# The last block of a hybrid decoder step: who weights, roots and scales the final rows

## The reference, cut to what matters

```python
def rmsnorm(x, g):
    return (_rms_f32(x) * g.astype(jnp.float32)).astype(x.dtype)   # x * rsqrt(mean(x*x) + EPS) * g

y = h + moe(hn, w_router, b_router, w_gate_up, b_gate_up, w_down, b_down)
y_prompt, y_sample = rmsnorm(y_prompt, g_final), rmsnorm(y_sample, g_final)
```

## Time and profile before

| | us |
|---|---|
| median of three runs | 1386.02 |
| the profiled execution, its own time | 1385.96 |
| its span, first to last instruction | 1384.1 |
| PE busy | 1352.9 (98%) |
| DVE busy | 1209.8 (87%) |
| ACT busy | 1091.7 (79%) |
| POOL busy | 1010.1 (73%) |

### The profile page before, as it was taken

How to read it: one execution, slowest core, us unless ns; L and a number is a source line. 1 busy time by engine, 2 the same in 40 slices (tenths; PEclk the granted TensorE clock), 3 DMA queues, 4 the chain that set the end, 5 groups by cost and what they waited for, 6 DMA issues and landing times.

```text
span 1384.1 us, 19701 instructions
## 1 busy us (share of the span) xinstructions
PE 1352.9 (98%) x6762; PEld 994.0 (72%) x6762; DVE 1209.8 (87%) x1092; ACT 1091.7 (79%) x1149; POOL 1010.1 (73%) x431
## 2 busy tenths in 40 slices
PE   8999999999999999999999999999999999999995
PEld 5988655667777777777777777777777777777773
DVE  5466556899999999999999999999999999999996
ACT  5354423778888888888888888888888888888885
POOL 2122211266699999899999998999999989999943
PEclk9999999999999999999999999999999999999998
DMA  9522272999999999999999999999999999999984
GB/s 354 189 66 72 88 276 70 367 394 356 372 351 377 378 369 382 372 392 379 377 393 373 378 382 375 379 384 365 389 380 365 381 390 374 382 371 386 375 313 150
DMA packets 51803, 458.99 MB, mean 332 GB/s; under 512 B 11450, under 2 KB 15516, under 8 KB 26122
## 3 DMA queue, kind: packets, MB, share of 16 engines
q1 hardware_dynamic: 40089, 438.33, 80.9%
q0 software_dynamic: 10000, 18.19, 6.0%
q10 hardware_dynamic: 1648, 1.65, 0.4%
HBM read 446.62 MB, written 22.08 MB: 339 GB/s over the span
## 4 chain that ended last, share of the span: by engine, by line
PE 77%; DMA 3%; DVE 1%; issue 1%; POOL 1%; ACT 0%; POOLq 0%; ACTq 0%; DVEq 0%
PE psum L2371 24%; PE psum L2373 24%; PE psum L2372 24%; DMA area<-hn_tbl,idx_i 3%; PE psum L2355 2%; PE psum L2366 2%; POOL small L810 0%; DVE low L1690 0%; PE psum L2342 0%; DVE area L1812 0%; POOL area L695 0%; DVE area L1772 0%; DVE ring L1836 0%; DVE area L1765 0%; POOL out L820 0%
## 5 line engine op out<-in xcount | busy, mean ns | idle before, releaser
L1690 DVE TENSOR_TENSOR low<-raw,high 128x2048 fp32r<-128x2048 f32 x384 | 875.1, 2310 | 35.9 <-ACT high L1098 35.8
L1098 ACT CAST high<-raw 128x2048 fp32r<-128x2048 f32 x384 | 727.8, 1913 | 23.7 <-PE psum L2373 19.2
L2371 PE MATMUL psum<-high,area_r 128*104 128x512 f32 x1536 | 610.4, 397 | 2.5 <-DVE area_r L1754 1.4
L2373 PE MATMUL psum<-low,area_r 128*104 128x512 f32 x1536 | 604.3, 393 | 0.0
L2372 PE MATMUL psum<-high,area_r 128*104 128x512 f32 x1536 | 603.9, 393 | 0.0
L668 POOL PARTITION_BROADCAST brow<-brow x192 | 382.8, 2074 | 41.1 <-DMA brow<-in_biases 40.6
L2373 PEld LDWEIGHTS psum<-low,area_r 128*104 128x104 f32 x1536 | 258.0, 168 | 96.5
L2371 PEld LDWEIGHTS psum<-high,area_r 128*104 128x104 f32 x1536 | 258.0, 168 | 95.0 <-DVE area_r L1754 1.6
L2372 PEld LDWEIGHTS psum<-high,area_r 128*104 128x104 f32 x1536 | 258.3, 168 | 90.7
L737 POOL DMA_INDIRECT area<-hn_tbl,idx_i x32 | 162.9, 5089 | 79.5 <-DVE idx_i L1657 40.8
L665 POOL COPY arrived<-cst 1x1 f32 x60 | 199.5, 3325 | 0.3
(11 more groups left out here) (269 smaller groups left out, 1175.5 us busy)
## 6 DMA issues: line engine op xcount, KB each, us to landing
raw<-in_w_gate_up SPq DMA_DIRECT2D x128, 2048.0 KB, 11.1
raw<-in_w_down SPq DMA_DIRECT2D x64, 2048.0 KB, 11.7
ring<-in_w_in SPq DMA_DIRECT2D x7, 1024.0 KB, 15.3
ring<-in_x_prompt SPq DMA_DIRECT2D x8, 512.0 KB, 9.7
ring<-in_w_out SPq DMA_DIRECT2D x7, 512.0 KB, 4.6
ring<-in_w_mem_kv SPq DMA_DIRECT2D x2, 1024.0 KB, 9.3
ring<-in_mem_kT SPq DMA_DIRECT2D x1, 2048.0 KB, 8.5
ring<-in_cache_mem_v SPq DMA_DIRECT2D x1, 2048.0 KB, 8.2
```

The costliest lines, as they stand in the source:

```text
L1098: nc.scalar.copy(high_w(i), raw_w(t)).then_inc(sem("w_high"), 1)
L1690: v.tensor_tensor(low_w(t), raw_w(t), high_w(i), ALU.subtract).then_inc(sem("w_low"), 1)
L2371: mm(bank, high, wh, start=False, stop=False, skip_group_check=True)
L2373: return mm(bank, high, wl, start=False, stop=stop, skip_group_check=True)
```

## The change

- POOL, between its gather and its roots, multiplies tiles 0 and 1 by `gfin` (128x1024 each); DVE no longer does.
- The five roots are three instructions: tile 2; tiles 3 and 4; tiles 0 and 1. For that `ssf` is set to 1 once, early in the program, so that unused rows of tile 4's column hold a number.
- DVE takes tile 2's mean ahead of `swiglu` of the second half, and scales tile 2 directly behind `swiglu`, ahead of `act_low` and the last `low` part. The means of tiles 0 and 1 stand together in front of the scaling of tiles 3 and 4.
- The last rows: DVE multiplies them by `gfin` into a new buffer `yw` while ACT squares; the scaling by the root is then shared, columns 0 to 511 by DVE, 512 to 1023 by ACT. The scatter waits for both.

```diff
 # ROOTS: first tile, behind the last tile, how many means must be there
+        ROOTS = ((2, 3, 1), (3, 5, 3), (0, 2, 5))
 # SP, store_rows
-                        sp.wait_ge(sem("yf_ready"), NTT * again + j + 1)
+                        sp.wait_ge(sem("yf_ready"), 3 * again + j - 1)
 # POOL, rows_last
-                for s, j in enumerate(ROW_ORDER):
-                    pool.wait_ge(sem("ssf_ready"), NTT * (times - 1) + s + 1)
-                    nc.gpsimd.tensor_tensor(rsf[0:ROWS[j], j:j + 1], ssf[0:ROWS[j], j:j + 1], mh[0:ROWS[j], 0:1],
+                for j in range(2):
+                    pool.wait_ge(sem(f"ld_y{j}"), 16 * times)
+                    nc.gpsimd.tensor_tensor(yg[j], yf[:, j, :], gfin, ALU.mult).then_inc(sem("yg_ready"), 1)
+                for first, last, ready in ROOTS:
+                    pool.wait_ge(sem("ssf_ready"), NTT * (times - 1) + ready)
+                    nc.gpsimd.tensor_tensor(rsf[:, first:last], ssf[:, first:last], mh[:, first:last],
                                             ALU.pow).then_inc(sem("rsf_ready"), 1)
 # ACT, last_squares
+                ac.wait_ge(sem("yw_ready"), 1)
+                ac.wait_ge(sem("rsl_ready"), 1)
+                nc.scalar.activation(yl[0:CAP, 512:1024], yw[0:CAP, 512:1024], ACT.Copy, scale=rsl[0:CAP, 0:1]).then_inc(sem("yl_half"), 1)
 # DVE, last_rows
+                dv.wait_ge(sem("yl_sum"), 2)
+                v.tensor_tensor(yw[0:CAP, :], yl[0:CAP, :], gfin[0:CAP], ALU.mult).then_inc(sem("yw_ready"), 1)
                 dv.wait_ge(sem("ssl_raw"), 2)
 ...
-                v.scalar_tensor_tensor(out=yl[0:CAP, :], in0=yl[0:CAP, :], scalar=rsl[0:CAP, 0:1], in1=gfin[0:CAP],
-                                       op0=ALU.mult, op1=ALU.mult).then_inc(sem("yl_ready"), 1)
+                v.tensor_scalar(yl[0:CAP, 0:512], yw[0:CAP, 0:512], rsl[0:CAP, 0:1], None, ALU.mult).then_inc(sem("yl_ready"), 1)
 # DVE, period, last
+                    if last and i == 6:
+                        row_means(2, 1)
                     if i == 6:
                         swiglu(n, 1)
                     if last and i == 6:
-                        row_means(2, 1)
-                        row_weights(0, 1)
-                        row_weights(1, 1)
+                        row_scale(2, 1)
```

More of the change, by code:

```diff
@@ L271, in build @@
         yl = view(ring, (NTT + 2) * D, [D])
+        yw = view(ring, (NTT + 3) * D, [D])
         yg = (xg[:, 1, :], yrow[:, 1, :])
         ROW_ORDER = (2, 3, 4, 0, 1)
+        ROOTS = ((2, 3, 1), (3, 5, 3), (0, 2, 5))
+        ROOT_OF = {j: i + 1 for i, (first, last, ready) in enumerate(ROOTS) for j in range(first, last)}
         wr = wr_t[:, :].rearrange("p (k e) -> p k e", k=KD)
@@ L819, in last_store @@
                 pool.wait_ge(sem("yl_ready"), 1)
+                pool.wait_ge(sem("yl_half"), 1)
                 nc.gpsimd.indirect_dma_start(y_out[:, :], last_slots, yl[0:CAP, :], None,
@@ L832, in _ @@
                         period(it * UB + (NE + u), u, overflow=True)
+                pool.wait_ge(sem("gathered"), (NE + EXTRA + 2) * 16)
                 rows_last(NE + EXTRA, 2)
@@ L1159, in row_root @@
             def row_root(j, times):
[L1161 to L1162 removed]
+                ac.wait_ge(sem("yg_ready"), 2 * (times - 1) + j + 1)
+                ac.wait_ge(sem("rsf_ready"), len(ROOTS) * (times - 1) + ROOT_OF[j])
                 nc.scalar.activation(yg[j], yg[j], ACT.Copy, scale=rsf[:, j:j + 1]).then_inc(sem("ssf_raw"), 1)
@@ L1539, in _ @@
                 v.tensor_copy(us[:, c, :, 0:2], src)
+            v.memset(ssf, 1.0)
             v.memset(eid_i[:, EXTRA:EXTRA + 1], 0).then_inc(sem("eid_zero"), 1)
@@ L1803, in row_scale @@
                 n = ROWS[j]
-                dv.wait_ge(sem("rsf_ready"), NTT * (times - 1) + ROW_ORDER.index(j) + 1)
+                dv.wait_ge(sem("rsf_ready"), len(ROOTS) * (times - 1) + ROOT_OF[j])
                 v.scalar_tensor_tensor(out=yf[0:n, j, :], in0=yf[0:n, j, :], scalar=rsf[0:n, j:j + 1], in1=gfin[0:n],
                                        op0=ALU.mult, op1=ALU.mult).then_inc(sem("yf_ready"), 1)
[L1808 to L1812, removed]
             def rows_final(times):
-                row_scale(2, times)
                 row_means(0, times)
+                row_means(1, times)
                 row_scale(3, times)
-                row_means(1, times)
                 row_scale(4, times)
@@ L1894, in _ @@
                 row_means(2, 2)
-                row_weights(0, 2)
-                row_weights(1, 2)
+                row_scale(2, 2)
                 row_means(3, 2)
```

## The result

The changed kernel takes 1394.21 us (median of six runs, 1391.85 to 1396.71), the kernel before on the same chip 1385.77 (six runs, 1385.04 to 1387.04). The ratio is 1.0063, 95% interval 1.0053 to 1.0073: slower by 8.4 us. On another chip it gave 1393.52 against 1385.79, ratio 1.0054 (1.0041 to 1.0068). The forecast was 1391.2 in a range of 1386.7 to 1393.0: the direction was right, the size 3 us too small. The profiled execution took 1394.27 us, span 1392.5.

The account below looks back on a forecast made before the run. The scatter's start was taken as the bound, set by the late stores and the last rows behind PE's last matmul. +5.8 (PE) +2.0 (clock) -1.3 (last rows) -1.2 (store path) gave +5.3: 1391.2 us, range 1386.7 to 1393.0.

Parts of the forecast that it names:

- PE restarts later: PE's restart for its last 24 matmuls, behind act_low: 1368.8 instead of 1363.01, +5.8 us.
- clock at half: PE's clock falls during its idle time and stays at half for 3 to 4 us: +2.0 us, lower bound 0.
- last rows: Weighting beside ACT's squares and scaling shared with ACT: 4.1 us instead of 5.4, -1.3 us, bounds 0 and -1.6.
- last rows ready to scatter: Store path before POOL's scatter, late before, now level with the last rows: -1.2 us.
- ahead of the stretch: Time before swiglu's last DVE instruction starts, from where runs are measured to the scatter's start: forecast 0.
- POOL is not free for 8.7 us: POOL stays occupied 8.7 us behind the configuration instruction after the gather; first multiplication at 1362.4.
- The multiplications: POOL's multiplications of tiles 0 and 1: 1.9 us each, 1362.4 to 1366.2; with 2.35 each, +0.9 us.
- first rival: POOL free before 1360.2: PE +3.5, idle 4.3 us, no clock fall; 1387.5 to 1388.6 us; chance 0.18.
- The store path: Stores of tiles 0 to 4 free the scatter at 1379.8 to 1381.0, level with last rows: -1.2 us.
- The memset: Setting ssf early on DVE, some 0.1 us where DVE is not the bound: nothing to +0.2 us.
- The rivals: POOL free before 1360.2: 1387.5 to 1388.6, 0.18; POOL taking DVE's port: 1386.0 to 1387.4, 0.09; root early: 1383.1 to 1383.8, 0.07.

Follow-up runs that it names:

- f1: The kernel before plus a tiny unused POOL multiplication ahead of the gather, so the configuration change stands there: 1385.84 us, ratio 0.9997.
- f2: The changed kernel plus a tiny unused POOL multiplication ahead of the gather, so the configuration change stands there: 1388.85 us, ratio 1.0026.
- g1: The changed kernel plus 27 unused small matmuls on PE ahead of its last 24 matmuls: 1392.23 us, ratio 1.0048.
- g0: The changed kernel run again, unaltered, on g1's chip: 1393.52 us, ratio 1.0054 to the kernel before.
- e2: The changed kernel with POOL taking tile 2's root ahead of its two multiplications: 1390.36 us, ratio 1.0028 to the kernel before.
- e4: The kernel before with only tile 2's scaling moved ahead of act_low: 1387.67 us, ratio 1.0014.
- h2: The changed kernel with its memset of ssf moved behind the routing: 1392.74 us, ratio 1.0047 to the kernel before.
- f3: The changed kernel plus 48 unused small matmuls on PE ahead of its last 24 matmuls: 1393.76 us, ratio 1.0058.
- h1: The kernel before with only the early memset of ssf added: 1385.94 us, ratio 1.0000.
- e1: The changed kernel with tile 2 scaled behind the last low part again: 1390.56 us, ratio 1.0034 to the kernel before.
- e3: The changed kernel with both gfin weightings back on DVE and tile 2 scaled behind the last low part: 1385.58 us, ratio 1.0000 to the kernel before.

## Why the prediction was too low

By its own steps, on the profiled execution (total +8.31 against +5.3 forecast):

| step | forecast | measured | how |
|---|---|---|---|
| PE restarts later | +5.8 | +5.92 | from L1775/L1787 to the restart: 3.58, then 9.50 |
| clock at half | +2.0 | +2.87 | first of the 24 matmuls to the last: 5.35, then 8.22 |
| last rows | -1.3 | -1.24 | 5.42, then 4.18 |
| last rows ready to scatter | -1.2 | -0.34 | 1.31, then 0.97 |
| ahead of the stretch | 0 | +1.24 | 1359.43, then 1360.67 |
| the rest | 0 | -0.14 | between these, and behind the scatter's start |

- **POOL is not free for 8.7 us.** Right in size and place: the first multiplication was 8.2 us behind the configuration instruction. The reason was wrong in its second half. I read the drain behind the scatter as the same picture and put the hold down to the indirect DMA. f1 and f2 show that it goes with the change of configuration. What the drain itself waits for, no run here shows. The forecast needed only the size, so this cost nothing here; it would have cost the cure, which is to place the configuration, not the gather.
- **The multiplications.** I took 1.9 us each by the row with a repeated operand; they took 2.34 with two full operands, the upper bound. Most of this +0.9 was offset: the first multiplication began 2.41 us behind the start of L1787, and I had assumed 1362.4-1359.43 = 2.97. That PE's restart came out at +5.92 for +5.8 is partly this luck.
- **The clock.** The mechanism was right and is shown by g1 (kept busy: 5.35 us, clock 1.00). The term was mis-sized: I took 3 to 4 us at half speed from the stretch at 248 to 251. Here the clock stayed at half for 6 us of PE's work, 15 matmuls at 0.43 instead of 0.23 us. g0 had 1.5 us, so a single value was never to be had; the range should have allowed 0 to 3. The idle time was no sure sign either: the prediction took the fall to come some 5.2 us into it, and it came 2.7 us into it here. Its first rival took an idle time of 4.3 us to be too short for a fall, and e2 fell with 3.92 us, while e4 did not with 3.46.
- **The last rows.** Right: weighting beside the squares and sharing the scaling saved 1.24 us of 5.42.
- **The store path.** This step failed. I took the scatter to follow 0.2 us behind the last rows once the stores were no longer late, and so gained 1.2; no row stood behind the 0.2. In the changed kernel it follows ACT's scaling by 0.97 us, with 0.60 and 0.25 us of POOL's own issuing in the chain, and by 0.97 in g0, h2 and f3 too. By the same 0.97 the store had been late by only 0.3 us before, not by 1.1. The other half of the step, when the stores free the scatter, was near: without the clock's fall they were to decide, at +4.2 us or more, and in g1 they did, at +5.55 (21.75-16.20).
- **The memset.** No cost seen (h1), within 1.2 us.
- **The rivals.** None happened in the changed kernel: its multiplications began at 1363.08 and ran while DVE waited. But the port is real and has a part in e1 and e2.

The miss of 3.0 us on the profiled execution is the clock (0.9), the store path (0.9) and the drift ahead of the stretch (1.24), which the sum put at nothing. The last has no cause shown and should have been in the range as scatter: its upper end, 1393.0, added only one of the open costs to the forecast.

What the change would give without its bad half is in e3: nothing that can be measured.

## What to carry to other kernels

Before work is given to an engine because it looks idle, read in the trace how long it needs from its last configuration change to its first ordinary instruction, and whether an in-order engine on the main path will stand behind the result. A wait put on DVE ahead of something that feeds PE can be paid twice, once as the wait and once as PE's lower clock behind it (in the changed kernel and e2, not in e4). When two paths end within 1 us of each other, shortening one brings the distance to the other and no more (e3, g1): measure the fixed part between the last wait and the last instruction before counting it as slack.

## What the runs showed of the hardware

- From a change of configuration behind the gather to POOL's first ordinary instruction it is 7.9 (e2) to 9.5 us (e4) in fourteen profiles, 8.2 in the changed kernel and 8.8 in the one before. It is 11.4 us in f1 and f2, where the change stands right behind an indirect add. A gather whose configuration is set ahead does not hold POOL that long: a multiplication ran 3.0 us after its start (f2).
- A 128x1024 multiplication on POOL takes 2.34 us with two full operands, 1.90 with a repeated one.
- A two-input DVE instruction and a POOL multiplication hold each other: 3.93 us instead of 2.27 for DVE and 6.80 instead of 4.65 for POOL's pair (e1), 3.38 instead of 1.28 for DVE (e2).
- The granted clock fell to half in the changed kernel at 1366.1, with PE idle since 1363.4, and in e2 at 1364.6, with PE idle since 1361.8. In h2 it fell 2.2 us and in g0 3.3 us into the idle time. In e4, with PE idle for 3.46 us, it did not fall, nor in g1, with PE idle for 0.90 us at most. Back at work, PE had it at half for 15 matmuls in the changed kernel, 12 in h2 and 8 in g0.
- In the changed kernel the scatter starts 0.97 us after the end of the last instruction that it waits for (ACT's scaling, 1383.05); the same 0.97 us lie there in g0, h2 and f3.
- The last store, 512 KB, landed 4.2 us (e3) to 6.1 us (the changed kernel) after its issue.
